# Hybrid diffusion step on one core: where the modulation blocks and the latent gate chunks stand on TensorE

## What is computed

```python
mod = silu(cond) @ w_ada + b_ada             # (6 x 1024) for each of 2 streams
shift1, scale1, gate1, shift2, scale2, gate2 = split(mod, 6)
h = rmsnorm(x, norm1) * (1 + scale1) + shift1
proj = h @ w_in     # conv gates bg, cg and values u; cq 256, ckv 128, kr 32; g_conv, g_mla
y_conv = (bg * conv3(cg * u)) @ w_conv_out
q = rmsnorm(cq, q_norm) @ w_uq;  kv = rmsnorm(ckv, kv_norm) ++ cache @ w_ukv   # 8 heads
y_mla = attention(q, kv) @ w_o
x = x + gate1 * ((sigmoid(g_conv) * y_conv + sigmoid(g_mla) * y_mla) @ w_mix_out)
h2 = rmsnorm(x, norm2) * (1 + scale2) + shift2
x = x + gate2 * moe(h2)                      # 32 experts, top 2 of one group of 8
y = rmsnorm(x, final_norm)
```

## Time and profile before

| | us |
|---|---|
| median of 3 runs | 1092.74 |
| lowest, highest run | 1091.93, 1094.31 |
| the profiled execution | 1093.69 |
| its span, first to last instruction | 1091.7 |
| TensorE busy | 917.6 (84%) |
| mean granted TensorE clock, of full speed | 0.928 |

### The profile page before, as it was taken

One profiled execution on the slowest core, in us unless ns is written; L12 is line 12 of the kernel. 1 busy time (PEld: TensorE's weight loads), 2 busy tenths in 40 slices (PEclk: granted clock), 3 DMA queues, 4 the chain that ended last, 5 costly groups with the idle time before them and its releaser, 6 DMA issues.

```text
span 1091.7 us, 14775 instructions
## 1 busy us (share of the span) xinstructions
PE 917.6 (84%) x5942; PEld 715.8 (66%) x5942; DVE 424.6 (39%) x839; ACT 269.0 (25%) x466; POOL 132.6 (12%) x193
## 2 busy tenths in 40 slices
PE   4669886999779999999999997639988878888566
PEld 3567553788779999999999886525444434444232
DVE  1644543344225252525223843552333332233224
ACT  5337543344321212121222312301111111111012
POOL 0000000010000000000000301212232323232220
PEclk9789996999889999999999998959999998899888
DMA  8601784221112222222312284557999999998856
GB/s 320 218 7 40 274 309 172 93 69 64 57 45 77 77 77 77 77 77 77 135 39 78 84 277 128 189 226 281 408 408 408 407 406 407 405 383 307 329 209 252
DMA packets 88141, 217.60 MB, mean 199 GB/s; under 512 B 11792, under 2 KB 43496, under 8 KB 87320
## 3 DMA queue, kind: packets, MB, share of 16 engines
q1 hardware_dynamic: 80824, 203.13, 50.5%
q0 software_dynamic: 7264, 13.74, 3.4%
HBM read 208.36 MB, written 18.43 MB: 208 GB/s over the span
## 4 chain that ended last, share of the span: by engine, by line
PE 60%; DMA 21%; DVE 8%; SPq 4%; issue 3%; ACT 2%; POOL 1%; POOLq 0%; DVEq 0%; ACTq 0%
DMA w_ug<-in_w_gate 12%; PE pair L1004 10%; PE pair L1008 10%; PE pair L1006 10%; PE pair L610 5%; DMA xg<-h_rows,at_g 4%; PE pair L997 4%; PE pair L998 4%; PE pair L999 4%; PE pair L1140 3%; PE pair L629 2%; PE pair L656 2%; SPq L411 2%; PE pair L1023 2%; PE pair L1162 2%
## 5 line engine op out<-in xcount | busy, mean ns | idle before, releaser
L610 PE MATMUL pair<-w_ug,xgT 128*64 128x256 f32 x1216 | 156.8, 416 | 39.6 <-DMA w_ug<-in_w_gate 38.5
L610 PEld LDWEIGHTS pair<-w_ug,xgT 128*64 128x64 f32 x1216 | 93.3, 150 | 90.3 <-issue 30.4
L1296 ACT CAST hi<-raw 128x2048 fp32r<-128x2048 f32 (+3 forms) x36 | 63.2, 1757 | 251.2 <-PE pair L1008 208.6
L1004 PE MATMUL pair<-hT,hi 128*128 128x320 f32 x512 | 117.8, 311 | 6.4 <-DVEq L1620 6.4
L1468 DVE TENSOR_TENSOR lo<-raw,hi 128x2048 fp32r<-128x2048 f32 (+3 forms) x36 | 78.5, 2180 | 113.6 <-ACT hi L1296 113.1
L1008 PE MATMUL pair<-hT,lo 128*128 128x320 f32 x512 | 117.5, 311 | 0.0
L1006 PE MATMUL pair<-hT,hi 128*128 128x320 f32 x512 | 117.5, 311 | 0.0
L1004 PEld LDWEIGHTS pair<-hT,hi 128*128 128x128 f32 x512 | 86.5, 190 | 6.6 <-DVEq L1620 6.6
L1006 PEld LDWEIGHTS pair<-hT,hi 128*128 128x128 f32 x512 | 86.5, 189 | 0.0
L1008 PEld LDWEIGHTS pair<-hT,lo 128*128 128x128 f32 x512 | 86.4, 189 | 0.0
L688 ACT ACTIVATE sa<-pair 64x256 f32<-64x256 f32 x38 | 14.4, 380 | 251.7 <-PE pair L610 251.7
(11 more groups left out here) (258 smaller groups left out, 1470.6 us busy)
## 6 DMA issues: line engine op xcount, KB each, us to landing
w_ug<-in_w_up SPq DMA_DIRECT2D x38, 1024.0 KB, 16.4
w_ug<-in_w_gate SPq DMA_DIRECT2D x38, 1024.0 KB, 19.0
w_dn<-in_w_down SPq DMA_DIRECT2D x38, 1024.0 KB, 18.2
raw<-in_w_in SPq DMA_DIRECT2D x20, 1024.0 KB, 5.3
ada_b<-in_w_ada SPq DMA_DIRECT2D x16, 1024.0 KB, 8.5
ada_a<-in_w_ada SPq DMA_DIRECT2D x8, 1024.0 KB, 10.0
ya<-expert_rows SPq DMA_DIRECT2D x5, 1024.0 KB, 8.9
raw<-in_w_conv_out SPq DMA_DIRECT2D x4, 1024.0 KB, 5.2
```

The costliest lines, as they stand in the source:

```text
L610: x = pe.matmul(bank[2 + d % 2][g * SL:(g + 1) * SL, 0:DE], xgT[d % 2][:, k, h * SL:(h + 1) * SL], w_ug[r][:, g, h, k, :], start=(n == 0), ...
L1004: pe.matmul(o, st[0], m[0], start=first, stop=False)
L1296: act.copy(hi[n % 2][:, 0:size], raw[n % 4][:, 0:size]).then_inc(hi_done, 1)
```

## The change

- `ada_a` has six buffers. Chunks 8 to 15 (blocks 2 and 3) join chunks 0 to 7 in them; chunks 8 to 11 are loaded before SP's wait for `s_hlo`, chunks 12 to 15 behind it. TensorE does the eight chunks behind the latent projection, ahead of its wait for `s_latn`; ScalarE copies the two blocks out, ahead of its copies of the latent transposes. Transposes of tiles 4 and 5 wait for those copies (same PSUM banks).
- `qn_b` and `kvn_b` move to the latent stage's memory, and their two loads behind the wait for `s_hlo`. The write of the rotary key into `kT` waits for chunk 15.
- Blocks 4 and 5 (chunks 16 to 23) stand at (0, 3), (0, 4), (1, 2), (1, 3). SP keeps the gate pieces behind chunk 19.
- Gate chunks stand in (2, 1) to (7, 2), 16 of 27 units; by the code's division these are (2,2), (2,4), then i = 1, 2 and 4 of heads 3 to 6, and (7,1), (7,2). The first two gate pieces are split at (1, 4), (2, 0) and (2, 1).
- Blocks 0 and 1 of the conv loop's first turn wait for neither `s_ol` nor `gm_copied` nor VectorE's clearing; block 2 does for the first two. The split of the conv loop's second piece falls inside the attention, ScalarE's at (7, 3) and VectorE's at (7, 4).

```diff
-    ada_a = [sb(f"ada_a{i}", [P, 2, D], scope=part0) for i in range(5)]
+    ada_a = [sb(f"ada_a{i}", [P, 2, D], scope=part0) for i in range(6)]
...
-    ada_turn = {(0, 3): 8, (0, 4): 10, (1, 2): 12, (1, 3): 14, (2, 0): 16, (2, 1): 18, (2, 4): 20, (3, 0): 22}
-    mod_turn = {(1, 0): 2, (1, 4): 3, (2, 2): 4, (3, 1): 5}
+    ada_turn = {(0, 3): 16, (0, 4): 18, (1, 2): 20, (1, 3): 22}
+    mod_turn = {(1, 0): 4, (1, 4): 5}
-    room = units[units.index((3, 3)):]
+    room = units[units.index((2, 1)):units.index((7, 3))]
...
+            if q < N_ADA2:
+                if q >= 6:
+                    sp.wait_ge(ada_used, q - 5)
...
-        sp.dma_start(qn_b[:, :], io["q_norm"].partition_broadcast(P)).then_inc(s_bc, 16)
-        sp.dma_start(kvn_b[:, :], io["kv_norm"].partition_broadcast(P)).then_inc(s_bc, 16)
...
+        for q in range(N_ADA1, 12):
+            ada(q)
         sp.wait_ge(s_hlo, KD)
+        sp.dma_start(qn_b[:, :], io["q_norm"].partition_broadcast(P)).then_inc(s_bc, 16)
+        sp.dma_start(kvn_b[:, :], io["kv_norm"].partition_broadcast(P)).then_inc(s_bc, 16)
...
-        for q in range(N_ADA1, N_ADA):
+        for q in range(12, N_ADA):
...
+        for q in range(N_ADA1, N_ADA2):
+            ada(q, bank[4 + q // 4][:, 0:256])
         pe.wait_ge(s_latn, NT)
         for i in range(NT + 1):
             b = bank[2 + i]
+            if i >= NT - 1:
+                pe.wait_ge(s_mod, i - 1)
...
-        pe.wait_ge(s_ol, NH)
-        pe.wait_ge(gm_copied, N_CHUNK)
         with pe.Fori(0, 4) as it:
...
                     if q == 2:
                         pe.wait_ge(gc_free, it * 2 + 1)
+                        pe.wait_ge(s_ol, NH)
+                        pe.wait_ge(gm_copied, N_CHUNK)
...
+        act.wait_ge(s_modT, 2)
+        for b in range(2, 4):
+            act.wait_ge(ada_used, 4 * b + 4)
+            act.copy(mod[b % 2][:, :], bank[4 + b][:, 0:256]).then_inc(s_mod, 1)
...
+        act.wait_ge(ada_used, N_ADA2)
...
-            if (h, i) == (3, 1):
+            if (h, i) == (1, 4):
                 act.wait_ge(ada_used, N_ADA)
                 split_hi(N_GM, PIECE)
-            if (h, i) == (3, 2):
+            if (h, i) == (2, 0):
                 split_hi(N_GM + 1, PIECE)
...
-        gm_out(N_CHUNK - 1)
-        split_hi(N_CONV + 1, PIECE)
...
+        dve.sem_inc(blk_free)
         top(0)
...
-            if (h, i) in ((3, 2), (3, 3)):
-                split_lo(N_GM + i - 2, PIECE)
+            if (h, i) in ((2, 0), (2, 1)):
+                split_lo(N_GM + i, PIECE)
...
-        split_lo(N_CONV + 1, PIECE)
...
-        dve.sem_inc(blk_free)
```

More of the change, by code:

```diff
@@ L161, in build @@
     rt = [sb(f"rt{i}", [P, NH, 2, 8], scope=part1) for i in range(4)]
+    qn_b = sb("qn_b", [P, QL], scope=part1)
+    kvn_b = sb("kvn_b", [P, KVL], scope=part1)
     part1.close()
@@ L170, in build @@
     V = sb("V", [P, NKT + 1, NH * VH], scope=part2)
-    qn_b = sb("qn_b", [P, QL], scope=part2)
-    kvn_b = sb("kvn_b", [P, KVL], scope=part2)
+    behind_v = sb("behind_v", [P, QL + KVL], scope=part2)
     behind = ExitStack()
@@ L260, in build @@
     mod_w = [sem(f"mod_rows_w{i}") for i in range(2)]
-    ada_a_in = [sem(f"ada_a_in{i}") for i in range(5)]
+    ada_a_in = [sem(f"ada_a_in{i}") for i in range(6)]
     ada_b_in = [sem(f"ada_b_in{i}") for i in range(4)]
@@ L327, in build @@
     POOL_LO = 5
-    N_ADA1, N_ADA = 8, 24
+    N_ADA1, N_ADA2, N_ADA = 8, 16, 24
     N_LAT, N_UQ, N_UKV, N_GM, N_CONV, N_G, N_O, N_MIX = 0, 2, 3, 4, 8, 24, 28, 32
     units = [(h, i) for h in range(NH) for i in range(NT)]
-    ada_turn = {(0, 3): 8, (0, 4): 10, (1, 2): 12, (1, 3): 14, (2, 0): 16, (2, 1): 18, (2, 4): 20, (3, 0): 22}
-    mod_turn = {(1, 0): 2, (1, 4): 3, (2, 2): 4, (3, 1): 5}
+    ada_turn = {(0, 3): 16, (0, 4): 18, (1, 2): 20, (1, 3): 22}
+    mod_turn = {(1, 0): 4, (1, 4): 5}
     N_CHUNK = 4 * KD // 2
-    room = units[units.index((3, 3)):]
+    room = units[units.index((2, 1)):units.index((7, 3))]
     gm_turn = {}
@@ L349, in ada_buf @@
     def ada_buf(q):
-        if q < N_ADA1:
-            return ada_a[q % 5], ada_a_in[q % 5], 16 * (q // 5 + 1)
-        return ada_b[(q - N_ADA1) % 4], ada_b_in[(q - N_ADA1) % 4], 16 * ((q - N_ADA1) // 4 + 1)
+        if q < N_ADA2:
+            return ada_a[q % 6], ada_a_in[q % 6], 16 * (q // 6 + 1)
+        return ada_b[q % 4], ada_b_in[q % 4], 16 * ((q - N_ADA2) // 4 + 1)
     def nth(j0, d):
@@ L911, in ada @@
             t, s_in, _ = ada_buf(q)
[L912 to L916, removed]
+            if q < N_ADA2:
+                if q >= 6:
+                    sp.wait_ge(ada_used, q - 5)
+            elif q < N_ADA2 + 4:
+                sp.wait_ge(piece_used, 3 if q == N_ADA2 else 4)
             else:
@@ L1393, in gm_out @@
             act.copy(gms[g % 2][:, :], bank[7][:, 0:HALF]).then_inc(gm_copied, 1)
+        act.sem_inc(gc_free)
         exps(0)
@@ L1419, in _ @@
         o_hi(NH - 1)
-        gm_out(N_CHUNK - 1)
-        split_hi(N_CONV + 1, PIECE)
-        act.wait_ge(s_ol, NH)
-        act.sem_inc(gc_free)
         with act.Fori(0, 4) as it:
@@ L1475, in mod_out @@
                 dve.wait_ge(mod_w[b % 2], 16)
-            elif b >= 2:
-                dve.wait_ge(s_modT, b - 1)
             dve.tensor_copy(mod[b % 2][:, :], src).then_inc(s_mod, 1)
```

## The result

| | before | after |
|---|---|---|
| median, us | 1093.53 (4 runs, 1091.93 to 1095.35) | 1058.82 (4 runs, 1055.17 to 1063.9) |
| ratio | | 0.9685, 95% interval 0.9637 to 0.9734 |
| profiled execution, us | 1093.69 | 1061.23 |
| its span, us | 1091.7 | 1059.1 |
| mean granted clock | 0.928 | 0.944 |

The change makes the kernel 3.2% faster. The forecast was 1060, in a range of 1050 to 1077.

The account below looks back on a forecast made before the run. TensorE was taken as the bound, with the end following the conv loop's start. Terms 2.5 + 0 + 1.2 + 8.6 + 7.5 + 3 + 5.2 + 3.5 + 1.3 = 32.8 us gave 1060, range 1050 to 1077.

Parts of the forecast that it names:

- What bounds it: Whole kernel: TensorE bounds it; everything behind the conv loop's start follows in fixed order, so the end gains what the start gains.
- The sixth buffer: In the head: chunk 5 goes out with the first five, block 1 ends one spacing earlier; gain 2.5 us, bounds 0 and 3.
- Eight chunks behind the projection: Behind the latent projection: 8.6 us of chunk work fits the 9.64 us wait for normalised rows; cost 0, bounds 0 and 8.6.
- the 1.2 entered for the clock: Latent transposes: no idle stretch, so the clock stays high; 2.2 us less work, 1.2 taken, bounds 0 and 2.2.
- Two blocks less and the clock: Attention: two blocks leaving heads 2 and 3 gain 8.6 us; fewer low-clock stretches gain 5.2 us, bounds 0 and 10.
- The wait for chunks 20 and 21: Attention: these chunks' loads come earlier, so 8.5 us of TensorE wait become 0 to 2; gain 7.5 us.
- The other waits: Attention: waits for probabilities and small ones fall from 14.4 to 10.3 us; 3 us gain taken, bounds -6 and 6.
- The drain: Between last value product and conv loop: 6.4 us wait becomes 2.9; gain 3.5 us, plus 1.3 for the low clock after it.
- A clock that doesn't follow: Rival: transposes and short score matmuls keep the clock where it was; gain 25.1, 1068 us, chance 13%.
- Late chunks: Rival: chunks 12 to 15 or 20 to 23 miss their slot, 8.5 us wait plus 4.1 low clock; 1072.5 us, chance 12%.
- Slower units: Rival: fourteen attention units without filler can't keep pace, each waiting 4.25 us; loss of 21, 1114 us, chance 3%.
- The absorbed gain: Rival: the experts' loads keep their time whatever the mixer does, so little reaches the end; 1092 us, chance 2%.

Follow-up runs that it names:

- the run with two free buffers: Changed kernel with modulation chunks 14 and 15 loaded into the free buffers raw0 and raw1: 1057.25 us (0.9674).
- The run with the order alone: Kernel before, with SP's four gate-piece loads moved from behind modulation chunk 19 to behind chunk 23: 1082.95 us (0.9906).
- the fourth edit: Changed kernel with chunks 14 and 15 in raw0/raw1, last split behind `o_lo`, gate pieces behind chunk 23, second gate piece split at (2,2), (2,4): 1046.16 us.
- the gate chunks from head 3: Changed kernel with its 16 gate chunks in 20 units, (3,3) to (7,2), in place of 27: 1058.94 us (0.9674).
- the last split behind `o_lo`: Changed kernel with the split of the conv loop's second piece moved from (7,3) and (7,4) to behind `o_hi` and `o_lo` of head 7: 1057.06 us (0.9694).
- the late conv loop: Changed kernel with the conv loop's two start waits and VectorE's release put back where they were before: 1064.07 us (0.9746).

## Why the prediction was right, point by point

- **What bounds it** held: the end follows the conv loop's start. It came 30.3 us sooner, the end of the span 32.6. The loop at full clock makes up the difference. The rule is not exact: from the load of gate1 to `h_rows` it took 50.7 to 53.9 us with the same code, by the clock at the mixing product.
- **The sixth buffer** was put at 2.5 us and is less. Block 1's last chunk starts 1.0 us sooner (33.95, not 34.99) and ends 1.9 sooner, at 35.0 and not at the 34.4 forecast, since it now runs at full clock; the projection's last matmul starts 1.9 sooner (65.94, not 67.80). By itself the edit gave 1.4 at the first scores. The step that was mis-sized is that the last chunk would take the landing of the one before it, one spacing sooner; the spacing was kept, but the line as a whole came only 1 us sooner. The hole in the DMA traffic is gone (414 GB/s from 23 to 25 us in place of 182); why no more than this came of it is open.
- **Eight chunks behind the projection** were put at 0 and cost 1.7 us: the gap from the projection's last matmul to the transposes grew from 10.0 to 11.7. From there to the first scores it took 32.4 us in place of 33.3, so of the 1.2 entered for the clock 0.9 came in this trace (31.1 to 31.2 us, the full 2.2, in the traces where the transposes start at full clock). The failed step is "what the data do": I let chunks 12 to 15 go out together at 54 us and overlooked that with six buffers chunk 14 needs chunk 8 used, which TensorE does only after the projection. The wait is in the diff shown (`ada_used`, q - 5), and the run with two free buffers shows it. In all, the first scores gained 1.9 - 1.7 + 0.9 = 1.1 us in place of 3.7.
- **Two blocks less and the clock** were 8.6 + 5.2 = 13.8. TensorE's busy time in the attention fell from 165.71 to 152.01, 13.7. The split between the two is counted work, not a run of its own.
- **The wait for chunks 20 and 21** was put at 7.5 of 8.5, and all of it went in this trace. The run with the order alone shows its cause. The 1 us held back was too little for executions at full clock at (1,2): there 2.3 to 2.6 us of it come back. TensorE's wait began at 161.07 and not at 160, which changes nothing in the sum.
- **The other waits** were put at 14.4 before and 10.3 (11.4 with the reserve) after. The 10.3 leaves out the 0.7 us ahead of the first scores, which the 14.4 holds. Measured, with this one and without the drain, they are 11.5, so the gain is 2.9 where 3 was taken: 2.27 and 1.58 at the two gate pieces against 2.8 and 1.6 expected, 2.07 at (6,3) against 2.1, 1.12 at (5,1) against 0.4.
- **The drain** was 0.87 + 1.57 = 2.4 against 2.9, and the loop began at full clock. So the 1.3 for its clock was half of what came: 785.98 - 783.65 = 2.3, all of it there at the load of gate1.
- **The rivals.** A clock that doesn't follow: not so, 0.92 to 0.95, and 0.99 with the fourth edit. Late chunks: partly so, at chunk 15, at a quarter of the price set. Slower units: excluded by the gate chunks from head 3. The absorbed gain: excluded, the end came as much sooner as the loop's start and more.

Inside the attention each large term came for the reason given. That the whole sum, 32.8, came within 0.2 us of the span's 32.6 is luck: 2.6 us too much ahead of the attention and 2.4 too little behind and in it nearly cancel, and the four runs of the changed kernel spread by 9 us around it.

## What to carry to other kernels

Where one queue carries loads for two consumers, read what lies ahead of the load that is waited for: moving 4 MB behind the urgent 4 MB gave 10 us for one line. Put weight splits and other long side work of the helper engines into units where the main engine has a filler, because a long wait costs its length and then clock: behind the waits of 4.25, 6.4 and 7.88 us of the kernel before, half clock cost another 2.8, 2.6 and 4.1 us. And when a ring gets more users, write down for each load which earlier use frees its buffer; the one that waits for work behind a barrier is the late one.

## What the runs showed of the hardware

The clock falls at different places in executions of nearly the same code. The stretch at (1,2), behind waits of 0.85 and 0.94 us, is low in eight of the twelve traces and at full clock in four. Five of the traces have the same code up to there, the changed kernel's: three are low (both of the kernel itself and the last split behind `o_lo`), two are not (the late conv loop, the gate chunks in fewer units). It costs about 3 us, less what it hides of waits for chunks, and is a part of why eight runs of one code spread by 0.8%. The mixing product, behind its wait of 2.04 us in every trace, is the same case: half clock in eight traces, full in four, for some 2 us.

The clock rises under transposes alone. In the kernel before, TensorE did nothing but transposes from 77.80 us on, after 9.64 us of waiting, and the granted clock rose among them. Windows of the transposes and of what follows (same columns as the earlier trace rows), and the timeline at the rise:

```profile
77.80:82.10 4.30, 4.30 (x20) 3.99 (x21) 2.96 (x8) 2.16 (x8) 1.32 (x2) 0.50 0.06 19
82.20:85.00 2.80, 2.46 (x15) 2.13 (x13) 1.63 (x6) 2.61 (x6) 0.00 (x0) 1.00 0.00 0
```
```profile
81.91 0.41 PE L1078 MATMUL pair<-cst,lat 128*32 128x128 f32 x1
82.12 0.31 PE L1077 MATMUL pair<-cst,lat 128*128 128x128 f32 x1
82.27 0.27 PE L1078 MATMUL pair<-cst,lat 128*32 128x128 f32 x1
```

The same durations stand in the head. From 15.9 us on TensorE did nothing but 40 transposes, after 11 us of waiting. By its groups of instructions from 16 to 19.5 us and from 21.5 to 22.7 us:

```profile
L1035 PE MATMUL pair<-cst,x_tok 128*128 128x128 f32 x17 | 3.9, 421 | 11.0 <-DVE x_tok L1489 11.0
```
```profile
L1035 PE MATMUL pair<-cst,x_tok 128*128 128x128 f32 x13 | 1.6, 273 | 0.0
```

They take 421 ns each at first and 273 later. The granted clock reads 1.00 in both stretches, so here only the durations speak: the latent transposes take 0.41 us at a granted 0.50 and 0.27 at 1.00. The rule of the Trainium skill against this term (TensorE: Matmul & The Clock Gate, Part 4: PE-mode transpose) does not agree with these rows, and the measurement decides.
